# First projection in three parts in place of four: blocks split into thick and thin, modulation spread evenly beside

## What is computed

```python
mod = silu(c) @ w_ada + b_ada                     # 2048 -> 12288, one row vector
sh_a, sc_a, gt_a, sh_f, sc_f, gt_f = split(mod, 6)
h = rmsnorm(x, norm_mix) * (1 + sc_a) + sh_a      # 256 x 2048
p = h @ w_in                                      # 2048 -> c_q, c_kv, k_pe, q, k, v, z, b, a, gates
# c_q, c_kv, k_pe -> latent attention (8 heads); q, k, v -> causal convolution of 4 taps, silu,
# l2 norm -> gated delta rule in chunks of 64; both outputs are gated, mixed and added to x
```

## Time and profile before

| | |
|---|---|
| median of 3 runs | 2919.57 us (2915.37 to 2921.55) |
| the profiled execution | 2918.03 us, span of its instructions 2916.2 us |
| TensorE busy | 96% of the span |
| VectorE busy | 71% |
| ScalarE busy | 45% |
| mean granted TensorE clock | 0.984 of full speed |
| moved by DMA | 565 MB |

### The profile page before, as it was taken

The page is one execution under the profiler, slowest core; times in us unless marked ns, Lnnn a source line. Parts: engine busy times, 40 slices in busy tenths (PEclk is TensorE's granted clock), DMA queues, the critical chain, the costliest instruction groups (busy, mean ns, idle before and its releaser), DMA issues.

```text
span 2916.2 us, 45565 instructions
## 1 busy us (share of the span) xinstructions
PE 2788.9 (96%) x18230; PEld 2503.9 (86%) x18230; DVE 2056.0 (71%) x3058; ACT 1303.8 (45%) x2009; POOL 230.9 (8%) x195
## 2 busy tenths in 40 slices
PE   6988999999999999999999999999989999999996
PEld 6987788999999888888888889888977888888885
DVE  7888885677687786555556679997566566575665
ACT  4445542332344544444444554344555444444443
POOL 0230000000001100000000080111120000000011
PEclk9999999999999999999999999999999999999998
DMA  9853255555687586555555554543434555555553
GB/s 393 313 219 128 95 175 173 188 188 181 209 310 276 201 298 241 185 187 188 188 188 189 189 183 160 171 152 129 153 129 166 188 188 187 189 188 188 188 185 111
DMA packets 158323, 565.41 MB, mean 194 GB/s; under 512 B 17568, under 2 KB 21920, under 8 KB 158112
## 3 DMA queue, kind: packets, MB, share of 16 engines
q1 hardware_dynamic: 158112, 562.50, 55.9%
HBM read 560.33 MB, written 2.10 MB: 193 GB/s over the span
## 4 chain that ended last, share of the span: by engine, by line
PE 81%; DVE 11%; ACT 3%; POOL 3%; issue 2%; DMA 1%; SPq 0%; DVEq 0%; ACTq 0%; POOLq 0%
PE BK L345 31%; PE BK L346 16%; PE BK L348 9%; PE BK L350 8%; PE BK L349 8%; DVE LO L617 3%; PE BK L429 2%; DVE ADA L613 1%; ACT HI L505 1%; DVE TV L712 1%; DVE B L824 1%; PE BK L355 1%; POOL SQ L867 1%; POOL SQ L865 1%; DVE B L671 1%
## 5 line engine op out<-in xcount | busy, mean ns | idle before, releaser
L345 PE MATMUL BK<-H,HI 128*128 128x512 f32 x4160 | 1465.4, 397 | 23.5 <-DVE LO L617 15.5
L505 ACT ACTIVATE HI<-RAW 128x1024 fp32r<-128x1024 f32 x825 | 874.5, 1060 | 1321.1 <-PE BK L346 712.9
L617 DVE TENSOR_TENSOR LO<-RAW,HI 128x1024 fp32r<-128x1024 f32 x825 | 1020.0, 1237 | 399.1 <-ACT HI L505 398.5
L346 PE MATMUL BK<-H,LO 128*128 128x256 f32 x4160 | 1166.1, 280 | 0.0
L345 PEld LDWEIGHTS BK<-H,HI 128*128 128x128 f32 x4160 | 782.7, 188 | 216.0 <-DVE LO L617 18.4
L348 PE MATMUL BK<-H,HI 128*128 128x256 f32 x2704 | 804.5, 298 | 34.8 <-DVE B L667 20.3
L346 PEld LDWEIGHTS BK<-H,LO 128*128 128x128 f32 x4160 | 787.0, 189 | 0.0
L349 PE MATMUL BK<-H,HI 128*128 128x256 f32 x2704 | 773.6, 286 | 0.0
L350 PE MATMUL BK<-H,LO 128*128 128x256 f32 x2704 | 773.3, 286 | 0.0
L348 PEld LDWEIGHTS BK<-H,HI 128*128 128x128 f32 x2704 | 526.9, 195 | 76.2 <-issue 37.9
L349 PEld LDWEIGHTS BK<-H,HI 128*128 128x128 f32 x2704 | 527.3, 195 | 1.5 <-issue 1.0
(11 more groups left out here) (231 smaller groups left out, 1691.3 us busy)
## 6 DMA issues: line engine op xcount, KB each, us to landing
RAW<-wst_dram SPq DMA_DIRECT2D x825, 512.0 KB, 3.4
RAW<-wada_dram SPq DMA_DIRECT2D x155, 512.0 KB, 4.6
EARLY<-wada_dram SPq DMA_DIRECT2D x37, 512.0 KB, 8.0
EARLY<-wst_dram SPq DMA_DIRECT2D x33, 512.0 KB, 6.8
X<-xT_dram SPq DMA_DIRECT2D x8, 512.0 KB, 8.9
B<-bias_dram SPq DMA_DIRECT2D x32, 128.0 KB, 3.2
out_dram<-X SPq DMA_DIRECT2D x4, 512.0 KB, 2.7
CN<-consts_dram SPq DMA_DIRECT2D x1, 840.0 KB, 8.3
```

The lines of the kernel that those rows point to most:

```text
L345: e.matmul(bk[:, :], hh, H[:, k, :], start=first, stop=False, skip_group_check=True)
L346: e.matmul(bk[:, 256:512], ll, H[:, k, 0:256], start=False, stop=last, skip_group_check=True).then_inc(S["tile"], 1)
L505: e.activation(HI[:, u % NHL, :], raw_at(slot), ACT.Copy).then_inc(S["hi"], 1)
L617: e.tensor_tensor(LO[:, u % NHL, :], raw_at(slot), HI[:, u % NHL, :].bitcast(f32), sub).then_inc(S["lo"], 1)
```

## The change

The early passes are three in place of four. All 34 blocks take rows 0-3 first. Then twenty blocks (`THICK`: eight of `Q03`, all of `Q47`) take rows 4-7, and fourteen (`THIN`: `CBLK` and four of `Q03`) take rows 4-11. In the last pass the thin blocks take rows 12-15 (four tiles each), the thick ones rows 8-15 (eight tiles each). The tiles multiplied are the same. The early units are 41 in place of 51, the last pass has 27 in place of 17.

The 48 modulation steps of groups 1 to 3 are spread evenly over the first 39 units, where they were put into the first twelve or so of each 17. The list of `kinds` from the 80th unit on is as before. `qkv_chain` is started after the fourth block of `Q03` in the last pass, where it was started after the twelfth.

```diff
--- before.py
+++ after.py
@@ -10,7 +10,7 @@
 N_ADA = 192
 WOUT_ORDER = [8, 9, 10, 11, 12, 0, 1, 2, 3, 4, 5, 6, 7, 13, 14, 15]
 GROUPS = 4
-ERA = 17
+EARLY_L, ADA_L = 41, 39
 HAND = 4
 TAPS = 4
 
@@ -889,20 +889,18 @@
             mbank = Ring(w, BANK[3:8])
 
             kinds = ["A"] * 16
-            for g in range(GROUPS - 1):
-                put = 0
-                for i in range(ERA):
-                    due = min(16, max(0, -(-16 * (i - 1) // (ERA - 5))))
-                    kinds += ["L"] + ["A"] * (due - put)
-                    put = due
-            put = 16 * GROUPS
+            put = 16
+            for i in range(EARLY_L):
+                due = 16 + min(48, 48 * (i + 1) // ADA_L)
+                kinds += ["L"] + ["A"] * (due - put)
+                put = due
             late_at = len(kinds) - 16
-            for i in range(ERA * (GROUPS - 1), N_TILES // 8):
+            for i in range(EARLY_L, N_TILES // 8):
                 due = min(N_ADA, put if i < 80 else 64 + (i - 80) * 3 // 4 if i < 208 else 160 + (max(i, 220) - 220) * 5 // 8)
                 kinds += ["L"] + ["A"] * max(0, due - put)
                 put = max(put, due)
             lin_at = [i for i, k in enumerate(kinds) if k == "L"]
-            early = 16 * GROUPS + ERA * (GROUPS - 1)
+            early = 16 * GROUPS + EARLY_L
             raw_free, raw_by = [None] * (NRAW + NEARLY), [-1] * (NRAW + NEARLY)
             raw_at_tok = []
             lo_tok, hi_tok, unit_pe = {}, {}, {}
@@ -1189,14 +1187,18 @@
                     yield
                 return f
 
-            def partial(ks):
-                for c, n in enumerate(CBLK + Q03 + Q47):
+            THIN = CBLK + Q03[0:4]
+            THICK = Q03[4:] + Q47
+
+            def partial(ns, ks):
+                for c, n in enumerate(ns):
                     first = ks[0] == 0
                     if first:
                         part_tok[n] = None
                     run(block(H1, h_tok, 0, "w_in", 0, n, ev_part(n, first, c % 2 == 1), ks))
-            for k in range(0, 12, 4):
-                partial(range(k, k + 4))
+            partial(THIN + THICK, range(0, 4))
+            partial(THICK, range(4, 8))
+            partial(THIN, range(4, 12))
             need(h_tok, 15)
 
             def half_of(n):
@@ -1342,18 +1344,20 @@
                 l2_tok[hg] = qkv_tok[j]
                 rs_busy[0] = False
 
-            LATE = range(12, 16)
+            def rest(n):
+                return range(12 if n in THIN else 8, 16)
             for j in range(8):
-                run(block(H1, h_tok, 0, "w_in", 0, j, ev_c(j), LATE))
-            run(block(H1, h_tok, 0, "w_in", 0, 8, ev_kpe, LATE))
-            run(block(H1, h_tok, 0, "w_in", 0, 41, ev_ba, LATE))
+                run(block(H1, h_tok, 0, "w_in", 0, j, ev_c(j), rest(j)))
+            run(block(H1, h_tok, 0, "w_in", 0, 8, ev_kpe, rest(8)))
+            run(block(H1, h_tok, 0, "w_in", 0, 41, ev_ba, rest(41)))
             later(scalars(), 16, 8)
             later(l2norm(0), 0, 6)
             for n in Q03:
-                run(block(H1, h_tok, 0, "w_in", 0, n, ev_qkv(n - 9), LATE))
-            later(qkv_chain(), 0, TAPS)
+                run(block(H1, h_tok, 0, "w_in", 0, n, ev_qkv(n - 9), rest(n)))
+                if n == Q03[3]:
+                    later(qkv_chain(), 0, TAPS)
             for n in Q47:
-                run(block(H1, h_tok, 0, "w_in", 0, n, ev_qkv(n - 9), LATE))
+                run(block(H1, h_tok, 0, "w_in", 0, n, ev_qkv(n - 9), rest(n)))
 
             while None in (cq_tok[7], RN["kpe"], lin_tok["ba"]):
                 w.force()
```

## The result

The change made the kernel slower by a little: 2928.3 us against 2918.7 (medians of ten runs each), ratio 1.0037 (95% interval 1.0024 to 1.0050; intervals stand in square brackets from here on). The profiled execution of after took 2922.01 us, that of before 2918.03.

The account below looks back on a forecast made before the run. VectorE was taken to bound passes two and three and the convolution chain, TensorE the rest from 388 us. Units 17 to 71 lose 17.2 us, attention returns 13.4: 3.8 more, median 2923.4 us, range 2908 to 2937.

Parts of the forecast that it names:

- Passes two and three, 85 us: Units 17 to 40: VectorE bounds with 81 us of work plus 4 us idle, 85 us in all.
- a miss costs up to 3 us: Modulation sums in units 17 to 40: late last rows hold TensorE's queue, costing up to 3 us.
- rival three: Last modulation group's rows come late, so the even spread fails: 3 to 5 us, 2928 us; chance 0.05.
- Nothing for both: Pass one's denser loads, and constants loaded earlier with five ring slots in place of thirteen: no added time.
- Thick stage, 87.5 us: Rows 8 to 15 of the twenty thick blocks: 77 us at 3.85 a unit, plus norm and scalars, 87.5 us.
- Units 68 to 71, 17.2 us: First attention up-projection units: four chain blocks remain, so 17.2 us as before the change.
- Before's sum, 200.7 us: Old kernel's time for the stretch matching units 17 to 71, against 217.9 us forecast after the change.
- Give-back, 25.4 - L with L = 12: Sixteen units, mostly attention, after unit 72: gain is 25.4 less TensorE's new loss L of 12, so 13.4 us.
- recurrence steps that move in are taken from later, where they cost TensorE the same: Attention stretch: recurrence steps moved into it cost TensorE as much as later, so they leave the gain of 13.4 us unchanged.
- One: Faster rival: attention runs at TensorE's pace and idle in passes two and three goes, 2910 us; chance 0.22.
- One b: Faster rival: each GpSimd part sum costs VectorE 1.29 us, so passes two and three gain 15 more, 2908; chance 0.03.
- Two: Slower rival: recurrence and attention together run out of banks and TensorE waits, L 25, 2936 us; chance 0.30.

Follow-up runs that it names:

- e5: Changed kernel with the load-slot collision removed, last modulation step two units earlier, sums one unit later in TensorE's queue: 2918.91 us, ratio 1.0006.
- e1: Changed kernel with the five late load slots begun at slot 1 in place of slot 0: 2921.64 us, ratio 1.0024.
- e2: Changed kernel with the convolution chain started after the twelfth Q03 block again, in place of the fourth: 2922.99 us, ratio 1.0036.
- e3: Changed kernel with the recurrence's first step 160 tiles (20 units) later, so behind attention: 2930.05 us, ratio 1.0061.
- e7: Kernel before the change with all early part sums on VectorE, none on GpSimd: 2916.67 us, ratio 1.0002.
- e6: Changed kernel with the convolution chain begun four tiles later: 2919.43 us, ratio 1.0006.
- e4: Kernel before the change with only the 48 modulation steps spread evenly over the first 49 of 51 early units: 2914.61 us, ratio 1.0010.
- e8: Changed kernel with the edits of e5 and e6 together: 2916.04 us, ratio 0.9993.
- e10: e8 with the convolution chain started after the last Q03 block in place of the fourth: 2916.01 us, ratio 1.0005.
- e11: e8 with all early part sums on VectorE, none on GpSimd: 2907.89 us, ratio 0.9979.

## Why the prediction held in its range and missed in its terms

**Passes two and three, 85 us: wrong by 6.4.** VectorE's sum was right (81 us of work; busy 81.09). The step that failed was "a miss costs up to 3 us" with the last rows "ready about two units ahead". I had given this mechanism (rival three) 0.05. Both sums waited, 3.7 us in all, and with the half clock and the queues behind them they cost 7: e5 puts the stage at 84.4 without them. VectorE, forecast over 93% busy, was 89% busy.

**"Nothing for both" on the slots: wrong in the mechanism, right in size.** There is a wait of 4.35 us, which I could have read from the list's length modulo 13; e1 shows that it was covered.

**Thick stage, 87.5 us: 3.6 too much.** The period was right (3.86 for 3.85). Twenty periods are 77.2 us, so the scalars and the norm added 6.7 us to the stage and not 10.5. The norm's TensorE part began only at 299.87 us, so that most of it fell one stage later, into the next point. Unit 68 began 16.7 us later than before, counted from unit 17, where 17 were forecast: the misses of the stages and of before's sum cancel.

**Units 68 to 71, 17.2 us "as before": wrong by 5.7.** I moved `l2norm(0)` and didn't ask where it ends: its matmuls now stand in TensorE's queue from 299.87 us on, the first waits 2.71 us there, and the clock of the stage is 0.91 in place of 1.00. These are rows of one execution; no run took this wait away alone. In e2, whose norm has its first matmul only at 332.38 us, behind these units, the four take 19.0 us at clock 1.00:

```profile
288.90:307.90 19.00, 17.19 (x109) 12.99 (x110) 17.56 (x35) 9.91 (x24) 0.00 (x0) 1.00 0.35 123
```

**Before's sum, 200.7 us: 4.9 short.** One `hi` row was counted twice, so all my boundaries from unit 48 on were a unit early. It cancelled in part, since the later window began a unit early as well. That window, 298.5 to 387.9 us, holds 360 narrow matmuls and 183 others: fifteen units, where I priced sixteen (384 and 170). The losses given for units 51 to 57 and 58 to 67, some 7 us each, are 8.0 and 9.6 by the same windows; nothing was worked out from them.

**Give-back, 25.4 - L with L = 12: 4.5 too little.** 17.9 us came back, which by that form is L = 7.5, below the 9 to 15 that I gave; with the window's own counts the form is 26.6 - L, and L 8.7. But L wasn't what failed. e3 shows attention without the chain and without the recurrence: 77.0 us for the sixteen units, where 64 + 12 = 76 "besides recurrence work" was forecast. The step that failed was "recurrence steps that move in are taken from later, where they cost TensorE the same". They did not cost the same: with the recurrence behind attention (e3) units 72 to 177 took 7.6 us more than with it inside (after), because its steps fill attention's waits and the other way round. That they fill them is read from the waits, 11.6 us on the links against 3.2. The recurrence began in unit 71 or 72, not near 74, and its sixteen units took 107.6 us with its work among them.

**The rivals.** One: more came back from attention than forecast, but the idle time of passes two and three grew. One b: refuted by e7 at its price; its reading of 1.29 us, and with it "not on the full size", was wrong, since that time holds the addition's own wait. Two: refuted by e3. Three: the mechanism that happened, at 7 us in place of the 3 to 5 that I gave it. The measured 2928.3 is within the range, 2.3 us outside the forecast's own 2918 to 2926, and on the slower side of the 0.2% line. The profiled pair lies 3.99 us apart, as forecast (3.8), but that is two misses of 4.5 us of opposite sign in one execution, and doesn't count as evidence for the terms: it was luck. The other 5.6 us of the medians stand in no trace, and their cause is open; e5 and e6, each of which is near level with before, don't say which edit they belong to.

## What to carry to other kernels

Where work is spread evenly beside an in-order engine, place its last step by the queue position of the instruction that consumes it, not by when the result is needed: here two waits of 1 to 2.5 us went with 7 us of loss, and ending the steps two units sooner and consuming them a unit later took it back. Overlapping two latency-bound chains (recurrence and attention) paid 7.6 us in one execution's trace, though both use the same engines; the medians don't separate it. Up to unit 178, e4 was 5.5 us and e8 14.4 us ahead of before in one execution's trace, and their medians moved by 2 us at most: say of a stage what the trace shows, and of the kernel only what the interval does.

## What was not expected of the hardware

A wait of TensorE of only 1.18 us, ahead of sixteen matmuls of one column each, was followed by the lower clock: from 125.9 to 131.8 us matmuls started 0.213 us apart, against 0.119 before and after. The lower clock came behind this sum in all five executions with that wait (after, e1, e2, e3, e6: 1.17 to 1.18 us) and in none of the four in which the sum didn't wait (e5, e8, e10, e11). It isn't peculiar to the sums. In after it also fell behind this wait for a `lo`:

```profile
165.22 0.38 PE L348 MATMUL BK<-H,HI 128*128 128x256 f32 x1 [1.80 <-DVE LO L617]
```

And behind the second sum, where the wait was 0.41 to 0.45 us, it fell in e8 and e11 and not in e5 and e10; what decided it there is open. The effect runs through whole kernels: in the timed runs the mean granted clock over the span was 0.985 for before (29 runs beside e1), 0.981 for after and for e1, 0.984 for e4. Over a span of 2916 us a difference of 0.004 is some 12 us of full clock, more than the change cost. Yet e5 stayed at 0.982 in the mean and e8 at 0.981, and both were level with before, so that the mean clock alone doesn't tell the time.
